# Scan levels of a blocked RWKV inverse: 32x32 tiles in place of 64x64 tiles with zeroed quarters

## The chip, the core and the metric

The kernel runs on one core of a Trainium2 chip. The metric is the device time of one execution, in microseconds (us); lower is better. The core has TensorE (PE, with its weight loads shown apart as PEld), VectorE (DVE), ScalarE (ACT), GpSimd (POOL) and SyncE (SP, which here only issues DMAs). Each engine works through its own list of instructions and waits for the others by semaphores. Instructions themselves come from memory too: the profile shows them as DMA packets of a queue of the kind "instruction".

## What is computed

Two transformer blocks run one after the other. The part that the change touches is the linear recurrence of the first layer (RWKV-7), over 1280 tokens (256 of context, 1024 latent), 8 heads of width 64, in both directions:

```python
def rwkv7_scan(r, decay, k, v, a_vec, b_vec, s0, reverse):
    def step(S, inp):
        r_t, w_t, k_t, v_t, a_t, b_t = inp
        sa = jnp.einsum('bhij,bhj->bhi', S, a_t)
        S = S * w_t[:, :, None, :] + sa[..., None] * b_t[:, :, None, :] + v_t[..., None] * k_t[:, :, None, :]
        return S, jnp.einsum('bhij,bhj->bhi', S, r_t)
```

The kernel does it in chunks of 64 tokens. Within a chunk the dependence of a token on the earlier ones is a triangular 64x64 matrix per head, and the kernel needs the inverse of identity minus that matrix. It builds the inverse by doubling: from blocks of 2x2 on the diagonal it goes to 4, 8, 16 and 32 (four levels), and then joins the two 32x32 halves of the chunk.

## The kernel before

The program is a list of phases with a barrier between them. `phase_scan` (line 668) is one of them. Its main loop has `NB` = 10 steps of 128 tokens, and one more that only finishes (n = 10). A step handles two chunks of 64 tokens (partitions 0 to 63 and 64 to 127), 8 heads (`j`) and 2 directions (`d`).

In each step the engines work on two things in turn: the new block n (`new`) and the running state of block n-1 (`old`). PE's order is fixed by the loop at its end: `gram` (token by token products, L765), `turn_v` and `turn_bk` (transposes, L773 and L783), `mask_v` (L794), then for each of the four levels `level_p` (L808) and `level_z` (L820), then `last_p` (L831) and `last_z` (L843) for the join. Between them stand the products of the old block: `state_w` (L861), `state_u` (L874) and `state_ys` (L892 and L897). All matrix products are in fp32.

The blocks on the diagonal at a level are at most 32x32. The partitions are four groups of 32; group c holds rows of half c % 2 of chunk c // 2. In `level_p` a matrix product takes 64 rows at a time: the stationary operand is `mD`, which is the 64x64 matrix `mB` with its two off-diagonal 32x32 quarters set to zero, so that one 64x64 tile acts as two independent 32x32 products. GpSimd makes `mD` (L948). In `level_z` the same holds for `Pm`, the masked result: VectorE writes it 64 wide, with the mask `lmh` (`sc_lm_halves`) that repeats the level's mask and zeroes the other quarter (L978). `level_add` (L986, L988) adds the product to `Z` and transposes it into `X`, in 32x32 squares.

So a level is: PE `level_p` for d = 0 and 1, VectorE `level_mask`, PE `level_z`, VectorE `level_add`, and on to the next level. `last_p` and `last_z` already use 32x32 tiles, with a `tile_position`.

SP loads the operands of block n+2 (`sc_ar`, `sc_bk`, `sc_vt`, 1280 KB for each direction) once block n-1 has released its buffers, some microseconds behind the second `state_ys` of a step.

Of the kernel before, what the change touches and what calls it, by code (L numbers as in the profile page):

```python
# [8 lines left out]
ALU = mybir.AluOpType  # L9
# [3 lines left out]
P = 128  # L13
# [9 lines left out]
CH = 64  # L23
# [639 lines left out]
def phase_scan(g):  # L663

    nc = g.nc
    NL = len(LEVELS)
# [3 lines left out]
             "mB", "mK", "z0", "Zbase", "X", "Pm", "Zadd", "zdiag", "zf", "Wev", "stmp", "snew", "y",  # L670
             "diag", "blocks", "Uev", "Vev", "BKev", "MVev", "Pev", "y1"]
    reps = {"gB": 2, "gK": 2, "mB": 2, "mK": 2, "trBK": 2, "BKev": 2, "P": NL, "Z": NL, "Pm": NL, "Zadd": NL, "X": NL + 1, "diag": 4,
# [3 lines left out]
    yst = {(d, b): g.sem(f"sc_stored{d}{b}") for d in range(2) for b in range(2)}  # L676
    levels_ready = g.sem("sc_level_masks")
    consts, zeroed = g.sem("sc_consts"), g.sem("sc_zeroed")

    def done(eng, x, d, n, r=None):  # L680

        k = reps.get(x, 1)
        eng.wait_ge(S[x, d], n * k + (k if r is None else r + 1))
# [9 lines left out]
    with ExitStack() as ctx:  # L693
        def sb(name, shape):
            return ctx.enter_context(nc.sbuf_tensor(f"sc_{name}", shape, F32))
        ar, bk, vt = sb("ar", [P, 3, 2, 4, 2, P]), sb("bk", [P, 2, 2, 4, 2, P]), sb("vt", [P, 2, 2, 4, P])
        mB, mK = sb("mB", [P, 2, 2, 8, 2, CH]), sb("mK", [P, 2, 2, 8, 2, CH])
        V, Bt, MV, Zf = sb("V", [P, 2, 2, BANK]), sb("Bt", [P, 2, 2, 2, BANK]), sb("MV", [P, 2, 2, BANK]), sb("Zf", [P, 2, 2, 8, CH])
        dg, Z, X, P5 = (sb(x, [P, 2, 8, 32]) for x in ("diag", "Z", "X", "P5"))
        mD, Pm = sb("mD", [P, 2, 8, CH]), sb("Pm", [P, 2, 8, CH])  # L700
        W, U = sb("W", [P, 2, BANK]), sb("U", [P, 2, BANK])
        St, tmp, y = sb("S", [P, 2, 4, CH]), sb("Stmp", [P, 2, 4, CH]), sb("y", [P, 2, 2, 4, P])
        m1, mx = sb("m1", [P, 2, 2, CH]), sb("mx", [P, 2, 2, 32])
        lmh = sb("lm_halves", [P, 2, NL, CH])
        lm, hm, am, eye = sb("lm", [P, 2, NL, 32]), sb("hm", [P, CH]), sb("am", [P, 2]), sb("eye", [P, 32])
        bA, bB, bC, bD = ([ctx.enter_context(nc.psum_tensor(f"sc_b{x}{d}", [P, BANK], F32)) for d in range(2)] for x in "ABCD")

        with nc.Block() as block:
# [35 lines left out]
            def _(pe):  # L744
# [53 lines left out]
                def level_p(n, l):  # L798
                    for d in range(2):
                        done(pe, "X", d, n, l)  # L800
                        if l == 0:
                            done(pe, "BKev", d, n, 1)
                            done(pe, "blocks", d, n)
                        settle()
                        for j in range(8):
                            for q in range(2):
                                c = half(q)
                                last = mm(bA[d][c, 32 * j:32 * j + 32], mD[c, d, j], X[c, d, j], start=True, stop=True)  # L808
                        last.then_inc(S["P", d], 1)

                def level_z(n, l):
                    for d in range(2):
                        done(pe, "Pm", d, n, l)
                        if l == 0:
                            done(pe, "MVev", d, n)
                        settle()
                        for j in range(8):
                            for q in range(2):
                                c = half(q)
                                last = mm(bB[d][c, 32 * j:32 * j + 32], Pm[c, d, j], Z[c, d, j], start=True, stop=True)  # L820
                        last.then_inc(S["Z", d], 1)
# [117 lines left out]

            @block.gpsimd  # L940
            def _(pool):
                pool.wait_ge(consts, 96)
                for n in range(NB):
                    for d in range(2):
                        done(pool, "mB", d, n)
                        if n:
                            done(pool, "P", d, n - 1, NL - 1)
                        nc.gpsimd.tensor_tensor(mD[:, d], mB[:, n % 2, d, :, 0], hm[:].unsqueeze(1).broadcast_to([P, 8, CH]),  # L948
                                                ALU.mult).then_inc(S["blocks", d], 1)

            @block.vector
            def _(dve):
# [22 lines left out]
                def level_mask(n, l):  # L975
                    for d in range(2):
                        done(dve, "P", d, n, l)
                        tt(Pm[:, d].rearrange("s j (a c) -> s j a c", a=2),  # L978
                           bA[d][:, 0:256].rearrange("s (j c) -> s j c", j=8).unsqueeze(2).broadcast_to([P, 8, 2, 32]),
                           lmh[:, d, l].rearrange("s (a c) -> s a c", a=2).unsqueeze(1).broadcast_to([P, 8, 2, 32]),  # L980
                           ALU.mult).then_inc(S["Pm", d], 1)

# [48 lines left out]
                dve.wait_ge(consts, 96)  # L1031
                for d in range(2):
                    tt(lmh[:, d].rearrange("s l (a c) -> s l a c", a=2), lm[:, d].unsqueeze(2).broadcast_to([P, NL, 2, 32]),
                       hm[:].rearrange("s (a c) -> s a c", a=2).unsqueeze(1).broadcast_to([P, NL, 2, 32]), ALU.mult).then_inc(levels_ready, 1)
                dve.wait_ge(levels_ready, 2)
                for n in range(NB + 1):
# [2266 lines left out]
```

## Time and profile before

| | us |
|---|---|
| median of 3 runs (lowest, highest) | 3682.78 (3677.57, 3697.24) |
| the profiled execution | 3688.47 |
| its span, from the first to the last instruction | 3686.7 |
| busy: PE, PEld, DVE, ACT, POOL | 3296.3, 2755.4, 1805.7, 1178.6, 393.9 |

The scan's steps take the stretch from 673 to some 1165 us of the span; the rest of the kernel is before and behind it and is not touched. Busy time of PE is the union of its matrix products; their ends are modelled, and neighbours overlap, so starts of instructions and stretches tell more than durations. "Idle before ... <-issue" means that the engine stood still though nothing that the profile shows held it back. A matrix product in fp32 appears in the trace as two weight loads (LDWEIGHTS) and two products (MATMUL).

### The profile page before, as it was taken

To read this page: it belongs to the slowest core of one execution; us is meant where nothing else is said; L and a number is where in the kernel's file an instruction comes from. 1 tells how busy PE (TensorE), PEld (TensorE's weight loads), DVE (VectorE), ACT (ScalarE), POOL (GpSimd) and SP (SyncE) were. 2 spreads that over 40 slices of the span, in tenths; PEclk is the share of its full clock that TensorE was granted. 3 is DMA by queue.
4 is the path that set the end of the run, shared out by engine and by line. 5 is a ranking of instruction groups with operands and counts; after the bars stand their busy time and mean duration, and the time that the engine had idled before them with its cause. 6 is when DMAs were issued, how large, how long until landed. Compare 5 with 4: busy or idle time off the path is not lost. (4 is left out here: it accounts for less than half of the span.)

```text
span 3686.7 us, 62343 instructions
## 1 busy us (share of the span) xinstructions
PE 3296.3 (89%) x27450; PEld 2755.4 (75%) x27450; DVE 1805.7 (49%) x2463; ACT 1178.6 (32%) x1648; POOL 393.9 (11%) x272
## 2 busy tenths in 40 slices
PE   5599999798986689897999989998777999999999
PEld 3488888688886479855899977776546788888887
DVE  6454455455653542253555534753443463636364
ACT  0444334222222322255444422542552211111111
POOL 0122221000000112110000012211102000000000
PEclk9799999778876899999999999999788999999999
DMA  8112231422212321324112013122002111111112
GB/s 346 43 70 101 105 125 72 122 72 72 72 43 94 131 92 46 117 85 173 57 59 63 31 61 126 47 78 94 29 18 86 52 40 57 42 56 43 54 45 76
DMA packets 145995, 294.53 MB, mean 80 GB/s; under 512 B 10048, under 2 KB 86976, under 8 KB 140224
## 3 DMA queue, kind: packets, MB, share of 16 engines
q1 hardware_dynamic: 126608, 212.95, 17.1%
q0 software_dynamic: 19120, 77.60, 6.2%
q8 instruction: 218, 3.57, 0.4%
q14 instruction: 49, 0.40, 0.0%
HBM read 211.22 MB, written 79.30 MB: 79 GB/s over the span
## 5 line engine op out<-in xcount | busy, mean ns | idle before, releaser
L60 PE MATMUL ev_ps<-h_hi,ev_w_hi 128*128 128x512 f32 (+1 forms) x792 | 288.5, 364 | 36.5 <-POOL ev_w_lo L360 35.2
L60 PE MATMUL ff_ps<-h_hi,ff_w_hi 128*128 128x512 f32 x768 | 300.1, 391 | 2.2 <-DVE ff_w_lo L3043 2.2
L61 PE MATMUL ff_ps<-h_lo,ff_w_hi 128*128 128x512 f32 x768 | 299.8, 390 | 0.0
L62 PE MATMUL ff_ps<-h_hi,ff_w_lo 128*128 128x512 f32 x768 | 299.7, 390 | 0.0
L62 PE MATMUL ev_ps<-h_hi,ev_w_lo 128*128 128x512 f32 (+1 forms) x792 | 281.1, 355 | 0.0
L61 PE MATMUL ev_ps<-h_lo,ev_w_hi 128*128 128x512 f32 (+1 forms) x792 | 281.1, 355 | 0.0
L3043 DVE TENSOR_TENSOR ff_w_lo<-ff_w,ff_w_hi 128x1024 fp32r<-128x1024 f32 (+1 forms) x80 | 89.5, 1119 | 339.5 <-ACT ff_w_hi L3018 339.5
L60 PEld LDWEIGHTS ev_ps<-h_hi,ev_w_hi 128*128 128x128 f32 x792 | 150.5, 190 | 75.1 <-POOL ev_w_lo L360 36.0
L3018 ACT ACTIVATE ff_w_hi<-ff_w 128x1024 fp32r<-128x1024 f32 (+1 forms) x80 | 78.0, 975 | 326.3 <-PE ff_ps L62 324.0
L60 PEld LDWEIGHTS ff_ps<-h_hi,ff_w_hi 128*128 128x128 f32 x768 | 144.8, 189 | 34.0 <-DVE ff_w_lo L3043 3.8
L62 PEld LDWEIGHTS ff_ps<-h_hi,ff_w_lo 128*128 128x128 f32 x768 | 144.8, 189 | 30.3
L61 PEld LDWEIGHTS ff_ps<-h_lo,ff_w_hi 128*128 128x128 f32 x768 | 144.9, 189 | 30.1
L61 PEld LDWEIGHTS ev_ps<-h_lo,ev_w_hi 128*128 128x128 f32 x792 | 150.6, 190 | 21.7 <-issue 1.7
L62 PEld LDWEIGHTS ev_ps<-h_hi,ev_w_lo 128*128 128x128 f32 x792 | 150.4, 190 | 21.2
L2861 ACT ACTIVATE ma_e<-ma_s,ma_nm 128x1280 f32<-128x1280 f32 x64 | 84.9, 1327 | 217.7 <-DVE ma_nm L2895 217.7
L2835 PE MATMUL ma_o<-ma_pt,ma_v 128*128 128x128 f32 x1280 | 153.2, 275 | 0.0
L60 PE MATMUL ff_ps<-ff_mid_hi,ff_w_hi 128*128 128x512 f32 x384 | 149.4, 389 | 0.0
L61 PE MATMUL ff_ps<-ff_mid_lo,ff_w_hi 128*128 128x512 f32 x384 | 149.4, 389 | 0.0
L62 PE MATMUL ff_ps<-ff_mid_hi,ff_w_lo 128*128 128x512 f32 x384 | 149.4, 389 | 0.0
L2835 PEld LDWEIGHTS ma_o<-ma_pt,ma_v 128*128 128x128 f32 x1280 | 147.9, 192 | 0.0
L360 POOL TENSOR_TENSOR ev_w_lo<-ev_w,ev_w_hi 128x1024 fp32r<-128x1024 f32 x33 | 92.3, 2798 | 367.1 <-ACT ev_w_hi L432 367.1
L3074 DVE SCALAR_TENSOR_TENSOR ff_acc<-ff_rows,cols,ff_acc 128x1023 f32<-128x1023 f32 x96 | 123.2, 1284 | 3.4
(501 smaller groups left out, 8065.7 us busy)
## 6 DMA issues: line engine op xcount, KB each, us to landing
ff_w<-in_w_up SPq DMA_DIRECT2D x48, 512.0 KB, 3.5
ev_w<-in_ev_w_in POOLq DMA_DIRECT2D x33, 512.0 KB, 3.9
ada_wt<-in_ada_w POOLq DMA_DIRECT2D x12, 1024.0 KB, 8.5
ada_wt<-in_ada_w SPq DMA_DIRECT2D x12, 1024.0 KB, 8.7
ff_w<-in_w_down SPq DMA_DIRECT2D x32, 384.0 KB, 3.0
ar<-ev_ar SPq DMA_DIRECT2D x8, 1280.0 KB, 5.4
bk<-ev_bk SPq DMA_DIRECT2D x8, 1280.0 KB, 8.0
sc_ar<-ar SPq DMA_DIRECT2D x20, 512.0 KB, 6.1
```

The lines of the kernel that those rows point to most:

```text
L60: nc.tensor.matmul(out, w_hi, x_hi, start=start, stop=False)
L61: nc.tensor.matmul(out, w_hi, x_lo, start=False, stop=False)
L62: return nc.tensor.matmul(out, w_lo, x_hi, start=False, stop=stop)
L360: nc.gpsimd.tensor_tensor(w_lo[:, n % 2], w[:], w_hi[:, n % 2].bitcast(F32), ALU.subtract).then_inc(w_lo_done, 1)
L2835: mm = nc.tensor.matmul(po[:, u % 2, 0:P], v[:, h % 2, t], pt[:, u % 2, t * P:t * P + P], start=t == 0, stop=t == NT - 1)
L2861: nc.scalar.activation(e[:, s % 2], ps[:, 0:T], ACT.Exp, bias=nm[:, s % 2:s % 2 + 1], accum_out=sm[:, s % 2:s % 2 + 1]).then_inc(exps, 1)
L3018: nc.scalar.activation(w_hi[:, n % 2, 0:kt(n)], w[:, n % 2, 0:kt(n)], ACT.Copy).then_inc(w_hi_done, 1)
L3043: nc.vector.tensor_tensor(w_lo[:, n % 2, 0:kt(n)], w[:, n % 2, 0:kt(n)], w_hi[:, n % 2, 0:kt(n)].bitcast(F32), ALU.subtract).then_inc(w_lo ...
L3074: nc.vector.scalar_tensor_tensor(out=acc[:, x, i:LAT], in0=rows[:, 0:LAT - i], scalar=tap[2 - i], in1=acc[:, x, i:LAT], op0=ALU.mult, op1= ...
```

## The change

`level_p` and `level_z` now run with 32x32 tiles, one for each of the four groups of partitions, at tile positions (0,0), (32,32), (64,64) and (96,96). `level_p` takes its stationary operand straight out of `mB` (the 32x32 quarter on the diagonal), so `mD`, GpSimd's part of the phase and its semaphore go. `level_mask` writes 32 columns for each head instead of 64, with the plain mask `lm`; the two instructions that built `lmh` before the loop go. The results are the same sums.

```diff
-        dg, Z, X, P5 = (sb(x, [P, 2, 8, 32]) for x in ("diag", "Z", "X", "P5"))
-        mD, Pm = sb("mD", [P, 2, 8, CH]), sb("Pm", [P, 2, 8, CH])
+        dg, Z, X, Pm, P5 = (sb(x, [P, 2, 8, 32]) for x in ("diag", "Z", "X", "Pm", "P5"))
...
                 def level_p(n, l):
...
-                            done(pe, "blocks", d, n)
                         settle()
                         for j in range(8):
-                            for q in range(2):
-                                c = half(q)
-                                last = mm(bA[d][c, 32 * j:32 * j + 32], mD[c, d, j], X[c, d, j], start=True, stop=True)
+                            for c in range(4):
+                                k, a = slice(32 * c, 32 * c + 32), 32 * (c % 2)
+                                last = mm(bA[d][k, 32 * j:32 * j + 32], mB[k, n % 2, d, j, 0, a:a + 32], X[k, d, j],
+                                          start=True, stop=True, tile_position=(32 * c, 32 * c))
...
                 def level_z(n, l):
...
                         for j in range(8):
-                            for q in range(2):
-                                c = half(q)
-                                last = mm(bB[d][c, 32 * j:32 * j + 32], Pm[c, d, j], Z[c, d, j], start=True, stop=True)
+                            for c in range(4):
+                                k = slice(32 * c, 32 * c + 32)
+                                last = mm(bB[d][k, 32 * j:32 * j + 32], Pm[k, d, j], Z[k, d, j],
+                                          start=True, stop=True, tile_position=(32 * c, 32 * c))
...
-            @block.gpsimd
-            def _(pool):
-                pool.wait_ge(consts, 96)
-                for n in range(NB):
-                    for d in range(2):
-                        done(pool, "mB", d, n)
-                        if n:
-                            done(pool, "P", d, n - 1, NL - 1)
-                        nc.gpsimd.tensor_tensor(mD[:, d], mB[:, n % 2, d, :, 0], hm[:].unsqueeze(1).broadcast_to([P, 8, CH]),
-                                                ALU.mult).then_inc(S["blocks", d], 1)
...
-                        tt(Pm[:, d].rearrange("s j (a c) -> s j a c", a=2),
-                           bA[d][:, 0:256].rearrange("s (j c) -> s j c", j=8).unsqueeze(2).broadcast_to([P, 8, 2, 32]),
-                           lmh[:, d, l].rearrange("s (a c) -> s a c", a=2).unsqueeze(1).broadcast_to([P, 8, 2, 32]),
-                           ALU.mult).then_inc(S["Pm", d], 1)
+                        tt(Pm[:, d], bA[d][:, 0:256].rearrange("s (j c) -> s j c", j=8),
+                           lm[:, d, l].unsqueeze(1).broadcast_to([P, 8, 32]), ALU.mult).then_inc(S["Pm", d], 1)
...
-                for d in range(2):
-                    tt(lmh[:, d].rearrange("s l (a c) -> s l a c", a=2), lm[:, d].unsqueeze(2).broadcast_to([P, NL, 2, 32]),
-                       hm[:].rearrange("s (a c) -> s a c", a=2).unsqueeze(1).broadcast_to([P, NL, 2, 32]), ALU.mult).then_inc(levels_ready, 1)
-                dve.wait_ge(levels_ready, 2)
```

PE's list in the first step (n = 0) before, from `mask_v` to `last_z`. The name ahead of the arrow is the tile written; the number at the end is how many calls of the product stand there.

```order
L794 MATMUL sc_bB<-sc_V,sc_mK 64x64 x32
L808 MATMUL sc_bA<-sc_X,sc_mD 64x32 x32
L820 MATMUL sc_bB<-sc_Z,sc_Pm 64x32 x32
L808 MATMUL sc_bA<-sc_X,sc_mD 64x32 x32
L820 MATMUL sc_bB<-sc_Z,sc_Pm 64x32 x32
L808 MATMUL sc_bA<-sc_X,sc_mD 64x32 x32
L820 MATMUL sc_bB<-sc_Z,sc_Pm 64x32 x32
L808 MATMUL sc_bA<-sc_X,sc_mD 64x32 x32
L820 MATMUL sc_bB<-sc_Z,sc_Pm 64x32 x32
L831 MATMUL sc_bA<-sc_X,sc_mB 32x32 x32
L843 MATMUL sc_bB<-sc_Z,sc_P 32x32 x32
```

And in the changed kernel, at the same place (its lines are numbered anew):

```order
L791 MATMUL sc_bB<-sc_V,sc_mK 64x64 x32
L804 MATMUL sc_bA<-sc_X,sc_mB 32x32 x64
L817 MATMUL sc_bB<-sc_Z,sc_Pm 32x32 x64
L804 MATMUL sc_bA<-sc_X,sc_mB 32x32 x64
L817 MATMUL sc_bB<-sc_Z,sc_Pm 32x32 x64
L804 MATMUL sc_bA<-sc_X,sc_mB 32x32 x64
L817 MATMUL sc_bB<-sc_Z,sc_Pm 32x32 x64
L804 MATMUL sc_bA<-sc_X,sc_mB 32x32 x64
L817 MATMUL sc_bB<-sc_Z,sc_Pm 32x32 x64
L829 MATMUL sc_bA<-sc_X,sc_mB 32x32 x32
L841 MATMUL sc_bB<-sc_Z,sc_P 32x32 x32
```

Nothing changes its place; each of the eight level products of a step has 64 calls in place of 32. VectorE's list before, from the start of the phase to the first level:

```order
L1030 MEMSET sc_S 128x512
L1033 TENSOR_TENSOR sc_lm_halves<-sc_lm,sc_hm 128x256 x2
L959 TENSOR_TENSOR sc_mB<-sc_bA,sc_m 128x512 x2
L959 TENSOR_TENSOR sc_mB<-sc_bB,sc_m 128x512 x2
L959 TENSOR_TENSOR sc_mK<-sc_bA,sc_m 128x512 x2
L959 TENSOR_TENSOR sc_mK<-sc_bB,sc_m 128x512 x2
L967 TENSOR_TENSOR sc_Z<-sc_diag,sc_mx 128x256 x2
L970 TENSOR_TENSOR sc_Z<-sc_Z,sc_eye 128x256 x2
L973 STREAM_TRANSPOSE sc_X<-sc_Z 128x256 x2
L978 TENSOR_TENSOR sc_Pm<-sc_bA,sc_lm_halves 128x512 x2
```

And in the changed kernel:

```order
L1015 MEMSET sc_S 128x512
L946 TENSOR_TENSOR sc_mB<-sc_bA,sc_m 128x512 x2
L946 TENSOR_TENSOR sc_mB<-sc_bB,sc_m 128x512 x2
L946 TENSOR_TENSOR sc_mK<-sc_bA,sc_m 128x512 x2
L946 TENSOR_TENSOR sc_mK<-sc_bB,sc_m 128x512 x2
L954 TENSOR_TENSOR sc_Z<-sc_diag,sc_mx 128x256 x2
L957 TENSOR_TENSOR sc_Z<-sc_Z,sc_eye 128x256 x2
L960 STREAM_TRANSPOSE sc_X<-sc_Z 128x256 x2
L965 TENSOR_TENSOR sc_Pm<-sc_bA,sc_lm 128x256 x2
```

Two instructions at the start are gone, and each write of `Pm` has 256 elements for each partition in place of 512.

## Rows read from the trace of the kernel before

**Rows 1.** The page: engines, and the granted clock in 40 slices of 92 us.

```profile
PE 3296.3 (89%) x27450; PEld 2755.4 (75%) x27450; DVE 1805.7 (49%) x2463; ACT 1178.6 (32%) x1648; POOL 393.9 (11%) x272
PE   5599999798986689897999989998777999999999
PEclk9799999778876899999999999999788999999999
```

**Rows 2.** Busy time by engine (with counts), clock and DMA of stretches of the scan.

```profile
core 0: us, PE busy (x) PEld busy (x) DVE busy (x) ACT busy (x) POOL busy (x), PEclk, DMA share, GB/s
675.00:1150.00 475.00, 429.26 (x12597) 412.30 (x12591) 278.30 (x604) 117.08 (x252) 25.06 (x20) 0.80 0.24 61
1084.90:1088.50 3.60, 3.04 (x128) 2.93 (x128) 1.39 (x5) 0.66 (x2) 0.00 (x0) 1.00 0.02 5
```

**Rows 3.** Groups of the scan, 675 to 1150 us: busy us, mean ns | idle before.

```profile
L820 PE MATMUL sc_bB<-sc_Z,sc_Pm 64*64 64x32 f32 x2560 | 104.6, 243 | 3.5 <-issue 3.3
L808 PE MATMUL sc_bA<-sc_X,sc_mD 64*64 64x32 f32 x2560 | 96.5, 234 | 12.7 <-DVE sc_X L988 12.5
L978 DVE TENSOR_TENSOR sc_Pm<-sc_bA,sc_lm_halves 128x512 f32<-128x512 f32 x80 | 55.2, 690 | 49.9 <-PE sc_bA L808 49.7
L986 DVE TENSOR_TENSOR sc_Z<-sc_Z,sc_bB 128x256 f32<-128x256 f32 x80 | 32.8, 410 | 44.7 <-PE sc_bB L820 44.4
L948 POOL TENSOR_TENSOR sc_mD<-sc_mB,sc_hm 128x512 f32<-128x512 f32 x20 | 25.1, 1271 | 452.2 <-DVE sc_mB L959 452.2
```

**Rows 4.** Timeline of PE: level products and the join (start, length, instructions).

```profile
735.73 2.05 PE L808 MATMUL sc_bA<-sc_X,sc_mD 64*64 64x32 f32 x64 [0.94 <-DVE sc_X L988]
739.17 3.62 PE L820 MATMUL sc_bB<-sc_Z,sc_Pm 64*64 64x32 f32 x64
901.69 0.69 PE L831 MATMUL sc_bA<-sc_X,sc_mB 32*32 32x32 f32 x32 [0.15 <-DVE sc_X L988]
1094.90 2.22 PE L831 MATMUL sc_bA<-sc_X,sc_mB 32*32 32x32 f32 x64
```

**Rows 5.** Durations of `level_p`'s products over the trace: ns minimum/median/maximum.

```profile
L808 PE MATMUL sc_bA<-sc_X,sc_mD x2560: 186/219/309, 685.5 to 1139.9; 64*64 64x32 f32 x197
```

**Rows 6.** DMA queues of the scan, 675 to 1150 us.

```profile
q8 instruction: 100, 1.64, 1.4%
sc_ar<-ar SPq DMA_DIRECT2D x16, 512.0 KB, 6.1
```

**Rows 7.** DMA of 1081 to 1091 us, in 40 slices of 0.25 us.

```profile
DMA  0000002000000000000020000000000000300000
q8 instruction: 3, 0.05, 2.0%
```

**Rows 8.** Timeline of PE at two of its stops.

```profile
1083.67 0.33 PE L892 MATMUL sc_bD<-sc_mK,sc_V 64*64 64x64 f32 x4
1084.97 0.29 PE L892 MATMUL sc_bD<-sc_U,sc_Bt 64*64 64x64 f32 x5 [0.98 <-issue]
1088.53 1.12 PE L820 MATMUL sc_bB<-sc_Z,sc_Pm 64*64 64x32 f32 x32 [0.51 <-issue]
```

**Rows 9.** Waits of PE's weight loads in the scan, 675 to 1150 us: total, times, longest.

```profile
PEld sc_bA L808 <- issue: 14.5, 23, 1.0
PEld sc_bA L765 <- issue: 14.3, 17, 3.1
```

**Rows 10.** DMA of 899 to 912 us, where a step's loads run.

```profile
q1 hardware_dynamic: 6259, 3.14, 95.4%
q8 instruction: 3, 0.05, 1.7%
```

**Rows 11.** Timeline: GpSimd's part of a step, and the step's first level product.

```profile
865.97 2.51 POOL L948 TENSOR_TENSOR sc_mD<-sc_mB,sc_hm 128x512 f32<-128x512 f32 x2 [46.71 <-DVE sc_mB L959]
...
877.38 1.83 PE L808 MATMUL sc_bA<-sc_X,sc_mD 64*64 64x32 f32 x58
```

More of the change, by code:

```diff
@@ L670, in phase_scan @@
              "mB", "mK", "z0", "Zbase", "X", "Pm", "Zadd", "zdiag", "zf", "Wev", "stmp", "snew", "y",
-             "diag", "blocks", "Uev", "Vev", "BKev", "MVev", "Pev", "y1"]
+             "diag", "Uev", "Vev", "BKev", "MVev", "Pev", "y1"]
     reps = {"gB": 2, "gK": 2, "mB": 2, "mK": 2, "trBK": 2, "BKev": 2, "P": NL, "Z": NL, "Pm": NL, "Zadd": NL, "X": NL + 1, "diag": 4,
@@ L676, in phase_scan @@
     yst = {(d, b): g.sem(f"sc_stored{d}{b}") for d in range(2) for b in range(2)}
-    levels_ready = g.sem("sc_level_masks")
     consts, zeroed = g.sem("sc_consts"), g.sem("sc_zeroed")
@@ L703, in phase_scan @@
         m1, mx = sb("m1", [P, 2, 2, CH]), sb("mx", [P, 2, 2, 32])
-        lmh = sb("lm_halves", [P, 2, NL, CH])
         lm, hm, am, eye = sb("lm", [P, 2, NL, 32]), sb("hm", [P, CH]), sb("am", [P, 2]), sb("eye", [P, 32])
```

## Prediction

> **What bounds the kernel now.** I read the page first: PE is busy 89% of the span, no other engine over half [rows 1]. Where the scan lies (673 to 1165 us) PE stays at 9 tenths, but its granted clock drops, so PE has work there that is not dense. Next the stretch as a whole and its groups: in 475 us PE has 429 us busy, VectorE 278, and the two level products alone make 201 us [rows 2, 3]. PE lost only 12.5 us to `X` ahead of `level_p` [rows 3]. So PE sets the time of the scan; the rest of the kernel is not touched.
>
> The question is what PE is bound by: the array, the rate at which it starts instructions, or the supply of instructions. The timeline gives the pace. Each fp32 call is two weight loads and two products. A level product of both directions is 64 of each: 2.05 us at full clock, 3.62 us at half [rows 4]. Less the last one's own time (219 ns in the median [rows 5]) that is 29 and, within 1 ns, 54 ns between starts. As it nearly doubles with half the clock, the array limits it. The join, in 32x32 tiles, starts 32 products in 0.69 us, some 16 ns apart, and at half clock 64 in 2.22 us, some 32 ns with the pause between the directions [rows 4]. It too uses two tiles at a time, so a 32x32 tile is free in about half the time of a 64x64 one.
>
> Then the supply. In the 475 us the trace has 12597 products and 12591 weight loads [rows 2] and 100 instruction packets of together 1.64 MB [rows 6]: 252 PE instructions for each packet of 16 KB. Semaphore instructions and lost records fill that up to 256. So one packet feeds 64 fp32 calls. At 1081 to 1091 us the DMA view has nothing else: three packets, in slices 7, 21 and 35, thus 14 slices or 3.5 us apart each time [rows 7]. Meanwhile PE stands still twice with nothing to wait for, and starts again at 1084.97 and 1088.53 us, each time some 2.4 us behind the start of a packet [rows 7, 8]. The starts are 3.56 us apart, and between them lie 128 products and 128 weight loads, exactly one packet [rows 2, 8]. I read it so: when PE enters a packet, the next one is asked for, and never more than one ahead. **A packet of 256 instructions cannot go by in less than some 3.5 us.** For level products that is 27.5 ns for each recorded product, just under the 29 that the array takes today, which is why it shows only in stops on "issue": 14.5 us ahead of L808, 14.3 ahead of L765 with a longest of 3.1 [rows 9].
>
> The Trainium skill ("Runtime: NRT & Kernel Launch", Instruction fetch mechanics) says that each engine's instruction memory is refilled in blocks of 16 KiB, 256 instructions, while the current page is executed, and that the crossing is mostly hidden. The trace agrees with the block and not with "hidden" in this phase. The same section of the Trainium skill gives PE 128 KiB, which would be eight blocks ahead; by that a fast stretch of 128 products would never stop, and the stops in this trace say otherwise.
>
> **The change part by part.** *Level products.* 32 more calls for each of 8 products in 10 steps: 2560 more calls, 10240 more PE instructions, 40 more packets: 140 in place of 100. Array time goes down: four 32x32 tiles at once, each at the pace of the join's, would give 8 ns between starts, 128 in 1.0 + 0.2 us where 2.05 stood. That is one bound: 80 products by -0.85 us, -68 us. The other is the supply: 128 products of both directions are 256 instructions, one packet, 3.5 us where 2.05 (3.62 at half clock) stood: at most +1.45 us by 80, +116 us. The stops are in the trace and the pace of 8 ns is nowhere, so I take the supply, and do the sum over the whole scan:
>
> - Floor: 140 packets by 3.53 us (between 3.5 and 3.56) is 494 us, against 475 for the 100 now (4.75 each): +19.
> - Loads. While a step's operands load, the queues are 95% taken for 13 us, and only 3 packets came through [rows 10], one after a stop of 3.1 us [rows 9]. In 13 us there could be 3.7. 8 such loads (16 of `sc_ar`, one a direction) lie in the scan [rows 6]. Each costs at least 0.7 packets, 2.5 us, and at most, with two gaps of about 6 us for 3.5 each, 5 us. Middle 3.75, by 8: +30. Today a part of it is hidden behind array-bound work; in the new kernel it adds to a supply that has no slack.
> - What is over the floor elsewhere today: 475 less 100 by 3.53 less the 30 is 92 us. It comes from half clock (29 to 54 ns in level products; I expect the like for gram, mask and state products) and from waits at the step's ends. A level product at half clock takes 13 ns by the array and is covered by its packet's 3.5 us. Waits for VectorE inside a level are covered too, as `Pm` of d = 0 is masked while PE does d = 1. What is left is gram, mask and state products at half clock and the wait for `mB`: I take a third, 30 us, with 0 and 60 as bounds.
>
> Sum: 494 + 30 + 30 = 554, +79 us.
>
> *`Pm` half as wide.* It falls from 690 ns to about the 410 of `level_add`, which reads as many elements of PSUM: 80 by 0.28, 22 us of VectorE [rows 3]. PE no longer waits on it, since the packet takes longer than the product and the mask together: 0. Were supply no bound, up to -22.
>
> *`mD` and its wait.* GpSimd's 20 by 1.27 us [rows 3] end at 868.5 us where the first level begins at 877.4 [rows 11]: 0, and nothing is late in its place, since `X` and the transposed operands already come behind it. *`lmh`.* Two small instructions ahead of the loop, where VectorE then still waits for PE: 0, at most -1. *Switching between tile sizes.* The join follows a level within 0.15 us [rows 4], and that includes the wait for `X`; 60 more switches cost at most 9 us, and nothing while instructions are short: 0. *SP* issues the same DMAs; the loads start when the second `state_ys` of a step is done, as before.
>
> The profiled execution took 3688.5 us, 5.7 more than the median. 3688.5 + 79 = 3767, and against the median **3762 us**.
>
> **The rivals.**
>
> *Faster: the array is the limit and instructions are always there.* Place: the eight level products. Price: -68 us, with the narrower `Pm` up to -22: about 3605 us. It decides if PE holds more than one packet ahead or the next comes in 1.3 us in place of 3.5. For it: the pace doubles with half the clock. Against: all stops on "issue", and their 3.56 us. 5%.
>
> The Trainium skill ("TensorE: Matmul & The Clock Gate", Part 3: Packing small matmuls) has tiles at different positions start about 4 ns apart, which would give even less than this rival's 8 ns. Nothing in this trace sustains such a pace.
>
> *No change: PE starts a product every 15 to 16 ns at best, and supply does not bind.* 128 by 15.5 is 2.0 us, what stood there before. What remains is a little of VectorE's 22 us: 3670 to 3685 us. For it: no group runs faster than the join's 16 ns. Against: the same stops. 6%.
>
> *Only the floor.* Load and clock costs vanish into the packets' time: +19 to +40, 3702 to 3725 us. For it: today's 92 us over the floor are mostly array time. 16%.
>
> *The clock falls too.* The array is busy for a third of a level's time, so PE may be granted half clock (1.2 GHz) through most of the scan (0.80 on average now [rows 2]). Then what is not a level product takes the full 60 us over the floor, and loads 40: +119, and with waits at the step's ends up to +150, 3800 to 3835 us. 18%.
>
> My forecast, supply with loads and some half clock (3725 to 3800), gets 55%.
>
> **How the numbers follow.** About 0.5% (18 us) is what a measurement can tell from no change. Faster: the first rival and a sliver of the second, 0.07. Same: 0.07, the second and the lowest end of the floor case. Slower: the rest, 0.86. The range leaves out the first two rivals and the far end of the clock case: 3702 to 3825 us. The likeliest one's own range is 3725 to 3800.
>
> **What the changed profile would show.** Instruction packets in the scan: 140. Their distance in the levels: 3.5 us, even, with a level product of 128 starts spread over some 3.5 us, or in bursts at 8 to 16 ns with stops on "issue" between them, which become PE's largest idle cause. `Pm` near 410 ns, and VectorE's wait for L804 much longer. PE's busy share in the scan falls from 0.90 to under 0.75. A step's length grows from 47.7 (10 steps in 477 us) to some 56 us. I am wrong if packets come closer than 3.4 us, if a level product takes under 1.5 us without stops, or if the scan grows by less than the floor's 19 us.

## The result, and the profile after

The changed kernel takes 3797.40 us (median of 4 runs, 3791.99 to 3803.68), the kernel before 3682.78: a ratio of 1.0305, with an interval of 1.0272 to 1.0339. The forecast was 3762 us and slower. The profiled executions took 3795.14 and 3688.47 us, so on their own time the change costs 107 us, where the sum said 79.

The page of the changed kernel, in the form of [rows 1]: busy time, instructions, and the granted clock in 40 slices.

```profile
PE 3265.8 (86%) x32570; PEld 2713.0 (72%) x32570; DVE 1784.2 (47%) x2461; ACT 1178.2 (31%) x1648; POOL 369.1 (10%) x252
...
PEclk8799999677666689999899999999888999999999
...
q8 instruction: 258, 4.23, 0.5%
```

PE has 5120 products more and 31 us less of busy time, yet the span grew. The granted clock is lower in the slices of the scan, the 8th to the 14th: 6 or 7 tenths, where it was 6 to 8. The scan as a whole, and a stretch of 7.2 us in the levels, in the columns of [rows 2]:

```profile
675.00:1266.00 591.00, 411.40 (x17872) 380.71 (x17876) 257.60 (x604) 118.22 (x254) 0.00 (x0) 0.70 0.20 52
...
884.00:891.20 7.20, 3.94 (x258) 3.56 (x262) 4.04 (x11) 0.66 (x2) 0.00 (x0) 1.00 0.06 17
```

The same count of VectorE instructions (604) that lay in 475 us now needs 591 (the second window holds 155 products more than the 5120 that were added, so it is a few us too long; the steps below are the exact comparison). PE's share of busy time fell from 0.90 to 0.70, and no other engine took its place: VectorE went from 278 to 258 us. In the short stretch the clock is full, and 258 products with 262 weight loads, two packets' worth, take 7.2 us. The array is busy for a little over half of it.

The groups of the scan, as in [rows 3] (busy us, mean ns | idle before, and what ended it), then the longest waits of the weight loads, as in [rows 9]:

```profile
L804 PE MATMUL sc_bA<-sc_X,sc_mB 32*32 32x32 f32 x5120 | 79.1, 218 | 58.7 <-issue 47.2 <-DVE sc_X L973 11.5
L817 PE MATMUL sc_bB<-sc_Z,sc_Pm 32*32 32x32 f32 x5120 | 77.8, 220 | 62.0 <-issue 61.9
...
L965 DVE TENSOR_TENSOR sc_Pm<-sc_bA,sc_lm 128x256 f32<-128x256 f32 x80 | 33.9, 423 | 93.4 <-PE sc_bA L804 93.4
L971 DVE TENSOR_TENSOR sc_Z<-sc_Z,sc_bB 128x256 f32<-128x256 f32 x80 | 33.1, 414 | 90.5 <-PE sc_bB L817 90.3
```

```profile
PEld sc_bB L817 <- issue: 66.2, 37, 4.7
PEld sc_bA L804 <- issue: 65.8, 65, 2.3
PEld sc_bA L762 <- issue: 31.2, 18, 19.0
PEld sc_bA L829 <- issue: 21.2, 16, 4.0
```

This is the change in two numbers. The level products were 201 us of busy time and are 157; the idle time ahead of them was 16 us and is 121, of which 109 ended on "issue", that is on nothing that another engine did. VectorE got its shorter `Pm` (423 ns for 690) and spends what it saved, and more, in waiting for PE: 93 and 91 us where it was 50 and 45. The 31.2 ahead of L762 hold one wait of 19.0 us at the scan's first product, which is no part of the change: in the kernel before it ends just ahead of the window of [rows 9].

The timeline of PE (start, length, instructions, idle before) in that stretch, and once at half clock:

```profile
885.61 0.82 PE L817 MATMUL sc_bB<-sc_Z,sc_Pm 32*32 32x32 f32 x66
887.63 0.74 PE L817 MATMUL sc_bB<-sc_Z,sc_Pm 32*32 32x32 f32 x62 [1.20 <-issue]
888.22 0.74 PE L804 MATMUL sc_bA<-sc_X,sc_mB 32*32 32x32 f32 x64
889.46 0.18 PE L804 MATMUL sc_bA<-sc_X,sc_mB 32*32 32x32 f32 x1 [0.49 <-DVE sc_X L973]
891.15 0.74 PE L804 MATMUL sc_bA<-sc_X,sc_mB 32*32 32x32 f32 x63 [1.50 <-issue]
```

```profile
869.88 1.86 PE L804 MATMUL sc_bA<-sc_X,sc_mB 32*32 32x32 f32 x122 [1.70 <-issue]
```

A level product is torn in two: 66 products, a stop of 1.20 us with nothing to wait for, 62 more, and then the same in the next one. Between the restarts at 887.63 and 891.15 lie 3.52 us and 62 + 64 + 1 = 127 products, one packet. Between the stops 64 products start within 0.74 us; less the last one's own 0.2 us that is 8.6 ns apart, the "8 ns" of the first rival. At half clock (0.50 from 869.9 to 871.7 us) 122 products take 1.86 us, 13.5 ns apart, and still stand behind a stop of 1.70 us. So the array does what the first rival said, and it is worth nothing: PE stops after each such burst with nothing to wait for.

The DMA view says when they come. First 814 to 830 us of the changed kernel, in 40 slices of 0.4 us:

```profile
DMA  0001000000001000000010000000010000000001
...
q8 instruction: 5, 0.08, 1.9%
```

Five packets, 9, 8, 9 and 10 slices apart, 3.6 us in the mean. No row of a view joins the packets with PE's stops over the whole scan, so it was counted from the starts in the trace: of 126 stops of PE and its weight loads together that are longer than 0.3 us, 75 end 2.2 to 2.7 us behind the start of an instruction packet, where chance would put one in eight, and they hold 113 of the 186 us of all. Where two such restarts follow within 5 us (37 times), 251 to 255 recorded products and weight loads lie between them, every time, and 3.76 us in the mean. That is the closest evidence for the supply of instructions: a slow array or a fixed cost of each start would not stop PE once in 256 instructions.

And the queues of the scan, 675 to 1266 us, beside [rows 6]:

```profile
q8 instruction: 141, 2.31, 1.6%
...
sc_ar<-ar SPq DMA_DIRECT2D x17, 512.0 KB, 6.5
```

141 packets in the window for 100 before. Nine steps, from the first product of the first step to the first of the tenth, went from 47.3 to 58.1 us each. The whole scan, from its first product to its last, went from 498.6 to 604.6 us: 106 us, the whole of the loss. The scan starts 4 us later than in the profile of before (677.05 for 673.04), but so it did in a further profile of the old program, at 677.31 (the first experiment): that is spread from ahead of the scan and not the change.

### The profile page after: what moved, and what is told of

The parts are those of the page before. It is cut to its first block and busy times, and to the rows that moved or that the text cites. A ratio compares the mean times of both kernels' runs of the same rounds, so it can differ in the third digit from the quotient of the medians.

```text
span 3793.4 us, 72522 instructions
## 1 busy us (share of the span) xinstructions
PE 3265.8 (86%) x32570; PEld 2713.0 (72%) x32570; DVE 1784.2 (47%) x2461; ACT 1178.2 (31%) x1648; POOL 369.1 (10%) x252
## 3 DMA queue, kind: packets, MB, share of 16 engines
q8 instruction: 258, 4.23, 0.5%
## 5 line engine op out<-in xcount | busy, mean ns | idle before, releaser
L817 PE MATMUL sc_bB<-sc_Z,sc_Pm 32*32 32x32 f32 x5120 | 77.8, 220 | 62.0 <-issue 61.9
L804 PE MATMUL sc_bA<-sc_X,sc_mB 32*32 32x32 f32 x5120 | 79.1, 218 | 58.7 <-issue 47.2
```

The source lines that it names most:

```text
L804: last = mm(bA[d][k, 32 * j:32 * j + 32], mB[k, n % 2, d, j, 0, a:a + 32], X[k, d, j], start=True, stop=True, tile_position=(32 * c, 32 * c))
L817: last = mm(bB[d][k, 32 * j:32 * j + 32], Pm[k, d, j], Z[k, d, j], start=True, stop=True, tile_position=(32 * c, 32 * c))
```

## The experiments

Theories. **A**: instruction supply. PE gets one packet of 256 instructions in some 3.5 us, one ahead, so that the time follows the count of PE's instructions. **B**: the small tiles themselves (their start, the switch to and from 64x64, banks they share). **C**: the clock, which fell to 0.70 in the scan. **D**: the loads of the next operands, which crowd out the packets. The expectations of some runs use two letters otherwise: C there is a fixed cost of each start of a product, and D that only the tiles' own time counts. The first falls with the bursts above, 64 products at 8.6 ns and then a stop, the second with the run on idle tiles. Every kernel was run beside the kernel before; ratios are against that.

### Empty instructions

Edit, ahead of each level call of the kernel before:

```diff
+                                for _ in range(4):
+                                    settle()
```

> The kernel before, unchanged in its products and tiles, with four empty PE instructions ahead of each call of the level products: 10240 more instructions, as many as the change adds, but no more array work. Theory A (instruction supply: a packet of 256 PE instructions cannot go by in under some 3.5 us): 140 packets in the scan, packets 3.5 us apart in the levels, and +95 to +125 us on before, as the changed kernel has (+114.6). Theory B (the 32x32 tiles themselves are slow: switching of tile size, or a fixed cost for each start of a product): the empty instructions cost little, 0 to +15 us.

3686.99 us, ratio 0.9994 (0.9979 to 1.0009). The test did not take place: the page has the same 218 instruction packets as before, so the empty instructions never reached the program. It tells nothing on A. What is left of it is the spread: the same program, timed as another, comes out within 0.2%.

### Only `level_p` in 32x32 tiles

```diff
@@ level_p of the kernel before; level_z as it was
-                            for q in range(2):
-                                c = half(q)
-                                last = mm(bA[d][c, 32 * j:32 * j + 32], mD[c, d, j], X[c, d, j], start=True, stop=True)
+                            for c in range(4):
+                                k, a = slice(32 * c, 32 * c + 32), 32 * (c % 2)
+                                last = mm(bA[d][k, 32 * j:32 * j + 32], mB[k, n % 2, d, j, 0, a:a + 32], X[k, d, j],
+                                          start=True, stop=True, tile_position=(32 * c, 32 * c))
```

> Only level_p in 32x32 tiles, straight out of mB; level_z as before in 64x64 tiles with the wide masked Pm. Half of the added instructions. Theory A: 120 packets in the scan and about half the loss, +45 to +65 us. Theory B: also about half if the cost is for each start (+57), but +100 or more if it is the switching of tile size, as level_p and level_z now differ and PE switches more often (16 switches a step in place of some 10).

3733.42 us, ratio 1.0122 (1.0101 to 1.0143): +45 us for half of the added calls. The queue of the scan (675 to 1200 us):

```profile
q8 instruction: 120, 1.97, 1.6%
```

20 packets more cost 2.2 us each, and the other 20 of the whole change some 3.4 each (the difference of the two ratios). That the first are cheaper fits A, if the packets catch up a little while `level_z` still runs at the array's 29 ns; no run shows the catching up by itself.

### The tiles alone, with the wide `Pm` and GpSimd's masks

```diff
@@ on the changed kernel, with mD, lmh, the wide Pm and the GpSimd block of before
-                                last = mm(bA[d][k, 32 * j:32 * j + 32], mB[k, n % 2, d, j, 0, a:a + 32], X[k, d, j],
+                                last = mm(bA[d][k, 32 * j:32 * j + 32], mD[k, d, j, a:a + 32], X[k, d, j],
...
-                                last = mm(bB[d][k, 32 * j:32 * j + 32], Pm[k, d, j], Z[k, d, j],
+                                last = mm(bB[d][k, 32 * j:32 * j + 32], Pm[k, d, j, a:a + 32], Z[k, d, j],
```

> Both level products in 32x32 tiles, but mD still made by GpSimd and Pm still written 64 wide by VectorE with the halves' mask. Theory A (PE is short of instructions, VectorE is covered): as the changed kernel within 0.3%, +105 to +125 us on before. Rival V (the narrower Pm gives back part of the loss, 0.28 us for each of 80 writes): 10 to 22 us slower than the changed kernel, +125 to +137 us on before.

3800.29 us, ratio 1.0308 (1.0289 to 1.0327), that of the whole change. The row of `Pm` in this kernel:

```profile
L980 DVE TENSOR_TENSOR sc_Pm<-sc_bA,sc_lm_halves 128x512 f32<-128x512 f32 x80 | 55.0, 690 | 85.0 <-PE sc_bA L808 84.9
```

690 ns and 55 us, as before, against 423 ns and 34 us in the changed kernel: 21 us of VectorE and 25 of GpSimd taken out move the end by nothing that can be measured (the two intervals leave some 10 us open). The zeros at the terms for `Pm`, `mD` and `lmh` hold.

### Small tiles at the old number of instructions

This kernel issues half the level calls, each with the operands of two heads side by side (64 columns). It leaves out the odd heads' own stationary operands.

```diff
@@ level_p of the changed kernel; level_z alike
-                        for j in range(8):
+                        for j in range(0, 8, 2):
-                                last = mm(bA[d][k, 32 * j:32 * j + 32], mB[k, n % 2, d, j, 0, a:a + 32], X[k, d, j],
+                                last = mm(bA[d][k, 32 * j:32 * j + 64], mB[k, n % 2, d, j, 0, a:a + 32], X[k, d, j:j + 2],
```

> The changed kernel, but a level call now takes one head's stationary 32x32 and the moving operand of two heads (64 columns), so there are as many calls as before the change. It leaves out the odd heads' own stationary operands, so their levels are not the reference's. Four tiles at once, each 128 cycles a product: by rate of the array 15 ns between starts, half of before's 29. Theory A: 100 packets, and 10 to 40 us faster than before, since the array has slack and only the supply's floor is left. Theory C (a start of a product costs 28 ns whatever the tile): within 10 us of before. Theory B with switching of tiles: slower than before by 20 us or more.

3663.98 us, ratio 0.9939 (0.9920 to 0.9958). Its products, and its timeline:

```profile
L804 PE MATMUL sc_bA<-sc_X,sc_mB 32*32 32x64 f32 x2560 | 55.2, 227 | 29.5 <-DVE sc_X L973 26.2 <-issue 1.1
L817 PE MATMUL sc_bB<-sc_Z,sc_Pm 32*32 32x64 f32 x2560 | 52.8, 227 | 17.0 <-issue 14.7 <-DVE sc_Pm L965 2.1
```

```profile
890.85 1.10 PE L817 MATMUL sc_bB<-sc_Z,sc_Pm 32*32 32x64 f32 x64 [0.32 <-DVE sc_Pm L965]
```

The same tiles, with the same switches between sizes, and the same columns in all as the changed kernel, but 40 packets fewer: 22 us faster than before where the change is 115 slower. PE's idle time ahead of L804 ends on VectorE again (26.2 us), not on "issue" (1.1); ahead of L817 14.7 us on "issue" are left. That refutes the tiles' size and the switches (B) as the cause of the loss. A cost of each start is halved here with the calls, so this run says nothing against that. It is no kernel that could be used, since a call has one stationary operand and the heads have each their own.

### More calls with the old tiles

```diff
@@ on the kernel before: one more product beside each, into the bank's unused half
+                                if l:
+                                    mm(bB[d][half(1 - q), 256 + 32 * j:288 + 32 * j], mD[c, d, j], X[c, d, j], start=True, stop=True)
...
+                                mm(bA[d][half(1 - q), 256 + 32 * j:288 + 32 * j], Pm[c, d, j], Z[c, d, j], start=True, stop=True)
```

These go to the two 64x64 tiles that the level products leave idle, 7 for each 8 of theirs: 8960 PE instructions, 35 packets.

> The kernel before with one more call beside each level call, in one of the two 64x64 tiles that the level products leave idle (rows of one half, columns of the other); its results go to unused columns of the other bank and nobody reads them. In 7 of the 8 products of a step (not in the first level_p): 8960 more PE instructions, 35 packets. Theory A (supply): 135 packets and 7/8 of the changed kernel's loss, +85 to +105 us. Rival D (the tiles' time is what counts and idle tiles are free): 4 tiles at 58 ns each are 15 ns between starts, 128 in 1.9 us, what 64 take now: within 10 us of before. Theory B (32x32 tiles are slow as such): also no change, since no tile is smaller.

3775.81 us, ratio 1.0231 (1.0188 to 1.0274), +87 us or 2.5 a packet. Groups of its scan:

```profile
L822 PE MATMUL sc_bA<-sc_Z,sc_Pm 64*64 64x32 f32 x2560 | 115.5, 247 | 19.1 <-issue 19.1
L823 PE MATMUL sc_bB<-sc_Z,sc_Pm 64*64 64x32 f32 x2560 | 113.5, 246 | 14.8 <-issue 14.6
L810 PE MATMUL sc_bA<-sc_X,sc_mD 64*64 64x32 f32 x2560 | 108.4, 240 | 21.4 <-issue 21.3
```

And its scan in the columns of [rows 2] (677 to 1240 us):

```profile
677.00:1240.00 563.00, 458.07 (x17104) 435.14 (x17104) 280.91 (x605) 117.49 (x252) 25.04 (x20) 0.78 0.21 54
```

No 32x32 tile in the levels, and the same loss for nearly the same number of instructions, with the idle time on "issue". The products of L822 and L820 hardly differ in recorded length (247 ns for 243 before; the ends are modelled). The granted clock is 0.78, near the 0.80 of before, so the loss does not need the low clock of the changed kernel either. This and the run before it are the pair that decides between A and B: each has what the other lacks.

### Semaphore instructions in place of products

```diff
@@ on the kernel before, ahead of each level call
+                                for _ in range(4):
+                                    pe.wait_ge(consts, 96)
+                                    settle()
```

> The kernel before with four semaphore instructions (waits that are long fulfilled) ahead of each level call: 10240 more PE instructions that are no products, 40 packets, the test that the empty instructions of e1_nops were meant to be (they never reached the program: its instruction packets stayed 218). Theory A: 140 packets, +95 to +120 us, if a semaphore instruction itself takes under some 14 ns. If each costs PE's sequencer more than that (30 ns would be 3.8 us a product), the loss is larger, up to +300 us, and the packets are further apart than 3.6 us. Rivals B and C (cost of tiles or of starts of products): 0, as there is no more product.

4665.99 us, ratio 1.2646 (1.2598 to 1.2695): +979 us for 10240 instructions, 96 ns each. A piece of its timeline:

```profile
1005.67 5.36 PE L811 MATMUL sc_bA<-sc_X,sc_mD 64*64 64x32 f32 x24 [0.17 <-issue]
```

24 products in 5.36 us, 223 ns apart. I had thought of them as cheap; a wait that is already met adds 96 ns to PE's time. In the levels every second instruction is now one, 128 in a packet, and these alone take 12 us, so that supply is never short. The run says nothing for or against A.

### Without the loads: changed kernel and kernel before

Both leave out the loads of blocks 2 to 9; the scan computes with the operands and decays of blocks 0 and 1 again.

```diff
-                    if n + 2 < NB:
-                        load(n + 2)
...
-                            pe.wait_ge(ld[d, n % 2], 48 * (n // 2 + 1))
+                            pe.wait_ge(ld[d, n % 2], 48)
```

> The changed kernel without the loads of blocks 2 to 9: every step uses the operands (and decays) of block 0 or 1 again, so the scan's sum is not the reference's. The loads' term of the forecast was 30 us (20 to 40) on top of a supply without slack. Theory A: 25 to 45 us faster than the changed kernel. Rival: the loads are hidden, within 10 us of it.

> The kernel before without the loads of blocks 2 to 9, with the same part of the computation left out. Theory A: the loads slow the same instruction packets here too, but part of it is hidden behind the array: 10 to 30 us faster than before, less than in the changed kernel. Rival: the gain is as large as there, or larger, so the loads do not explain any of the change's loss.

The changed kernel takes 3768.53 us without them (ratio 1.0215, 1.0177 to 1.0254), 29 less than with them; the kernel before 3662.87 (0.9936, 0.9917 to 0.9954), 24 less. The scan of the changed kernel without loads (675 to 1238 us), in the columns of [rows 2], with its instruction packets, and then the queues of the kernel before without loads (675 to 1126 us):

```profile
675.00:1238.00 563.00, 412.17 (x17924) 381.61 (x17918) 257.05 (x604) 118.55 (x254) 0.00 (x0) 0.72 0.06 16
...
q8 instruction: 142, 2.33, 1.7%
```

```profile
q1 hardware_dynamic: 13836, 6.89, 5.8%
q8 instruction: 101, 1.65, 1.4%
```

By the medians the loads cost the changed kernel some 5 us more than the old one, less than the intervals can tell from none; from the scan's first product to its last it is 27 us (604.6 less 577.3) in the changed kernel and 31 (498.6 less 467.7) in the old. So they cost either kernel something near 25 to 30 us. Without any load at hand the change still costs 106 us (3768.53 less 3662.87). D is no cause of the loss. The counts of packets stay as they were, 142 in 563 us and 101 in 451, and the queue that carries the operands is down to 5.8%.

### The added calls once more

```diff
@@ level_z of the changed kernel, each product issued twice
+                                mm(bB[d][k, 32 * j:32 * j + 32], Pm[k, d, j], Z[k, d, j],
+                                   start=True, stop=True, tile_position=(32 * c, 32 * c))
```

> The changed kernel with every call of level_z issued twice in a row (same operands, same result): 10240 more PE instructions, 40 more packets, 180 in the scan. What the forecast mis-sized is the packet's floor: 3.53 us was used, and the changed kernel's packets outside the loads lie 3.78 us apart in the median and 3.96 on average. Theory A with 3.53: +141 us on the changed kernel; with the measured 3.8 to 4.0: +150 to +160, that is +260 to +275 on before. Rival (first packets are cheap, slack remains): as the first 40, +115 on the changed kernel. Array alone (8.6 ns a product at full clock): 128 more products a level_z are 1.1 us by 40, +44.

3952.00 us, ratio 1.0720 (1.0699 to 1.0740): 154.6 us over the changed kernel for 40 packets, 3.87 each. Its DMA from 1000 to 1020 us, in 40 slices of 0.5 us, and its timeline at one stop:

```profile
DMA  0000001000000010000001000000001000000100
```

```profile
1000.00 0.23 PE L819 MATMUL sc_bB<-sc_Z,sc_Pm 32*32 32x32 f32 x3
1002.23 0.25 PE L817 MATMUL sc_bB<-sc_Z,sc_Pm 32*32 32x32 f32 x4 [2.00 <-issue]
```

Packets 8, 7, 9 and 7 slices apart, 3.9 us in the mean, with nothing else on the queues, and PE stands for 2 us of that. By the array alone 5120 products at 8.6 to 13.5 ns would have cost 44 to 69 us.

Not all of the 154.6 us lie in the scan. The first products of the scan and the last ones, in the changed kernel and then in this one (count: ns minimum/median/maximum, first and last start):

```profile
L762 PE MATMUL sc_bA<-sc_ar,sc_bk x640: 266/414/473, 677.0 to 1206.9; 64*64 64x128 f32 x160
L895 PE MATMUL sc_bC<-sc_ar,sc_S x640: 213/218/364, 736.5 to 1281.7; 64*64 64x64 f32 x160
```

```profile
L762 PE MATMUL sc_bA<-sc_ar,sc_bk x640: 268/296/472, 678.8 to 1343.3; 64*64 64x128 f32 x160
L897 PE MATMUL sc_bC<-sc_ar,sc_S x640: 213/218/364, 751.8 to 1430.7; 64*64 64x64 f32 x160
```

The scan takes 752 us for 605: 147 more, **3.7 us** a packet. The other 10 us between the two profiles (spans of 3950.2 and 3793.4) stand ahead of and behind the scan, where the programs are the same; even with them the price is 3.9. So 3.7 is the price of a packet where there is no slack left. The packets of the changed kernel say the same: where the queues carry no loads and a round (from 1.1 us ahead of a packet's start, where PE restarts, to the same point of the next) holds products of the levels alone, the starts are 3.7 us apart in the mean (27 rounds, 3.34 to 4.14).

### The same calls with nearly twice the array's work

```diff
@@ level_p of the changed kernel; level_z alike. The second 32 columns are overwritten by the next call
+                            v = 2 if j < 7 else 1
-                                last = mm(bA[d][k, 32 * j:32 * j + 32], mB[k, n % 2, d, j, 0, a:a + 32], X[k, d, j],
+                                last = mm(bA[d][k, 32 * j:32 * j + 32 * v], mB[k, n % 2, d, j, 0, a:a + 32], X[k, d, j:j + v],
```

> The changed kernel with the same number of calls, but each level call's moving operand is 64 columns wide (the next head's columns come along, and the next call overwrites them), so the array works about twice as long for a level and its results are the same. Theory A: a product then takes a tile as long as before the change (15 ns between starts on four tiles, 1.9 us for 128), still under a packet's 3.6 us: within 10 us of the changed kernel. If the granted clock rises because the array is busier, up to 15 us faster through the products that are not of the levels. Rival (the levels are bound by the array or by the tiles): +40 us or more on the changed kernel.

3802.81 us, ratio 1.0315 (1.0288 to 1.0342): that of the changed kernel. Its scan, and PE at one stop:

```profile
675.00:1266.00 591.00, 419.60 (x17776) 387.01 (x17776) 258.53 (x604) 118.06 (x254) 0.00 (x0) 0.87 0.21 53
```

```profile
888.00 0.98 PE L819 MATMUL sc_bB<-sc_Z,sc_Pm 32*32 32x64 f32 x56 [0.93 <-issue]
```

The granted clock is 0.87 where it was 0.70, and the scan is as long. More work in the array gave the clock back, and the two together did not move the end. Alone this would leave room for a trade, more work in the levels against a faster clock elsewhere; the run on the idle tiles closes it, as it has the loss at the clock of before (0.78 for 0.80). C is out as the cause of the loss: the low clock is a sign that PE stands still. The array is not the bound of the levels, as a nearly doubled cost went into the stops.

The clock does count where the array binds, in the `gram` of a step. The stretch of its 128 products, with 32 of its neighbours, at full clock (in the run at the old count) and in the changed kernel, in the columns of [rows 2]:

```profile
714.40:720.30 5.90, 4.61 (x160) 4.28 (x160) 4.07 (x9) 1.77 (x5) 0.00 (x0) 1.00 0.02 4
```

```profile
785.00:792.00 7.00, 6.28 (x160) 6.15 (x160) 4.32 (x9) 1.75 (x5) 0.00 (x0) 0.66 0.01 2
```

About 1.1 us a step, and no part of the loss: from its first start to its last `gram` takes 7.9 us in the mean of ten steps before and 7.1 in the changed kernel.

## Why the prediction was right, and where it was off

*What bounds it.* Right. In the levels a packet of 256 instructions takes longer to come than the array needs for it. Shown from four sides: PE's long stops end behind a packet and one packet apart, the loss follows the instruction count in small tiles (+20 packets +45 us, +40 +115, +80 +265) and in large ones (+35, +87), it is gone with the count (small tiles at the old count -22), and it does not change when the array's work nearly doubles. That PE never holds more than one packet ahead is the simplest reading of this and was not tested by itself. The Trainium skill ("Runtime: NRT & Kernel Launch", Instruction fetch mechanics) has blocks of 16 KiB and 256 instructions; the 40 packets for 10240 instructions, and their 0.66 MB (4.23 less 3.57), agree. Its remark that the refill is mostly hidden does not hold in this scan, where PE stands 109 us on "issue" ahead of the level products.

*Level products.* The bound taken, the supply's, was the right one; the other (-68 us) would have needed instructions at once. The run at the old count gives -22 us against the old kernel, with VectorE's `X` as the next wait and some of the supply's stops still there; what the small tiles would be worth with no limit of supply at all no run shows.

*Floor: the term that was mis-sized.* 140 packets were put at 3.53 us, a number from two restarts at the best place of the old trace. Where nothing but level products runs, packets come 3.7 us apart in the mean, and forty further packets lengthened the scan by 3.7 us each. 140 by 3.7 is 518 us, 24 more than the 494 in the sum: most of the miss of 28 us (107 between the profiles, 79 in the sum). The medians lie 115 us apart; the 8 us more are the spread of the two profiled executions. Over all rounds outside of loads the starts of the packets, which were taken one by one from the changed kernel's trace and which no row of a view shows, are 3.96 us apart in the mean, 3.78 in the median and 3.34 at the least; that mean is higher since it holds the rounds of `gram`, where the array takes longer than the packet. The prediction named a distance under 3.4 us as its refutation; 3 of 112 rounds come so close. What spreads the rounds of level products from 3.34 to 4.14 us with idle queues stays open.

*Loads.* The term was right: 30 us (20 to 40) foreseen, 29 measured by the medians and 27 in the scan. The remark that a part of it "is hidden today" does not show: the old kernel pays 24 by the medians and 31 in the scan.

*Over the floor elsewhere.* 30 us, a third of 92, had been kept for half clock and waits. On the basis of the forecast the scan now takes 475 + 106 = 581; less 518 and 27 to 29 that leaves 34 to 36. That is a remainder and no measurement of its own, but the size was about right, and the largest part of it can be named: a stretch of `gram` holds 160 products, one packet and a quarter, for which the supply would need 4.6 us, and it takes 7.0. Ten times 2.4 is 24 us, an estimate from the rows above. "A third" itself had no reason, so that it fits is in part luck.

*The terms at zero.* `Pm`, `mD` and GpSimd, `lmh`: confirmed together, by the run that keeps them all. Tile switches: the run at the old count has them all and is faster than before, so they are small, though not measured alone.

*Rivals.* "Start at 15 to 16 ns" falls with the 8.6 ns between stops. "Array" had that pace right, and falls with the stops. "Only the floor" (3702 to 3725) falls because the floor is higher and the loads do cost their 27 to 29 us on top. "The clock falls too" came nearest to the number (3800 to 3835) and has the wrong cause: the clock did fall, from 0.80 to 0.70, but where it costs time, in `gram`, it costs no more than before. A forecast from that case would have been nearer by luck.

*Signs.* 140 packets: yes. Bursts at 8 to 16 ns and stops on "issue" as PE's largest idle cause: yes. `Pm` near 410 ns: 423. Busy share under 0.75: 0.70. A step of some 56 us: 58.1.

## What to carry to other kernels

Count an engine's instructions before its array time: where a stretch has 256 PE instructions (here 64 fp32 calls, each two weight loads and two products) in less than about 3.7 us, splitting a call into more and smaller ones lengthens it, however well the pieces fit in the array. The signs are idle time on "issue" with instruction packets landing at even distances on otherwise idle queues; take the mean of many such distances as the price, since two at the best place gave a floor 5% too low here. Small tiles paid here only where the number of calls stayed the same, and a low granted clock beside such stops can be their result and not a cause, as it was here.

## What the runs showed that I had not expected

- A semaphore wait that is already met costs PE 96 ns (979 us for 10240), more than three times the 29 ns (3.7 us by 128) that a recorded product with its weight load costs in supply; an empty instruction without a wait does not reach the program at all.
- Four 32x32 tiles sustain starts 8.6 ns apart in bursts of 64 at full clock, 13.5 ns at half: 1.6 times as far, where the 29 and 54 ns of the two 64x64 tiles are 1.9 times. The Trainium skill ("TensorE: Matmul & The Clock Gate", Part 3: Packing small matmuls) has starts about 4 ns apart at different positions. No run here shows these; 8.6 ns is the closest.
- Nearly twice the columns in the same number of calls raised the granted clock of the scan from 0.70 to 0.87, at no change in time.
- A packet's price grows with their number: in the scan, from its first product to its last, 2.3 us for the first 20, 2.5 for 35, 2.7 for 40, 3.7 for the forty after these. The likely reason, not tested by itself, is slack that array-bound stretches had left.
